# Recurrence levels in two groups of four matrix pairs instead of four groups of two

## What is computed

```
decay = jnp.exp(jnp.where(incl, gc[..., :, None] - gc[..., None, :], -jnp.inf))
lower = jnp.where(strict, bc[..., :, None] * kk * decay, 0.0)
sol = lax.linalg.triangular_solve(jnp.eye(CHUNK, dtype=f32) + lower, rhs, ...)
...
u = u_c - w_c @ S;  o = qd_c @ S + qk_c @ u;  S = exp(ge_c) * S + kd_c.T @ u
```

## Time and profile before

| | |
|---|---|
| median of 3 runs | 3671.87 us (3669.95 to 3673.09) |
| the profiled execution | 3669.49 us, its span 3667.7 us |
| busy in the span | PE 92%, PEld 76%, DVE 72%, ACT 53%, POOL 17% |
| mean granted TensorE clock | 0.957 of full speed |
| the recurrence | 284.7 to 565.0 us of the span |

### The profile page before, as it was taken

One profiled execution on the slowest core, in us unless ns is written; L12 is line 12 of the kernel. 1 busy time (PEld: TensorE's weight loads), 2 busy tenths in 40 slices (PEclk: granted clock), 3 DMA queues, 4 the chain that ended last, 5 costly groups with the idle time before them and its releaser, 6 DMA issues. The chain is left out here.

```text
span 3667.7 us, 46334 instructions
## 1 busy us (share of the span) xinstructions
PE 3362.4 (92%) x16708; PEld 2778.2 (76%) x16708; DVE 2648.5 (72%) x3181; ACT 1954.2 (53%) x2670; POOL 619.2 (17%) x605
## 2 busy tenths in 40 slices
PE   4998998998699999999999986888999988889999
PEld 2778997776588888888888873777787767768877
DVE  4777774965699999999999986786775246753323
ACT  4535543322588888888888863275322234743222
POOL 1006770000010101011010103184000013710000
PEclk8998999999799999999999997989999999999999
DMA  5318114852699999999999966501565322023322
GB/s 180 107 64 316 36 36 157 292 163 110 251 369 380 375 386 373 388 377 386 376 381 381 376 269 211 164 35 47 172 200 156 98 83 39 35 67 94 97 94 69
DMA packets 290590, 750.92 MB, mean 205 GB/s; under 512 B 35528, under 2 KB 161160, under 8 KB 237434
## 3 DMA queue, kind: packets, MB, share of 16 engines
q1 hardware_dynamic: 277068, 694.43, 52.5%
q0 software_dynamic: 8480, 36.71, 2.8%
q10 hardware_dynamic: 4896, 17.83, 1.2%
HBM read 697.40 MB, written 57.01 MB: 206 GB/s over the span
## 5 line engine op out<-in xcount | busy, mean ns | idle before, releaser
L2548 DVE TENSOR_TENSOR ex_WP_lo<-ex_W,ex_WP_hi 128x2048 fp32r<-128x2048 f32 x408 | 918.7, 2286 | 43.7 <-ACT ex_WP_hi L2472 39.2
L2472 ACT CAST ex_WP_hi<-ex_W 128x2048 fp32r<-128x2048 f32 x408 | 766.1, 1909 | 198.2 <-PE PS L73 173.5
L71 PE MATMUL PS<-ex_WP_hi,ex_xT_hi 128*128 128x512 f32 x1056 | 418.7, 396 | 11.2 <-DVE ex_xT_lo L2557 5.8
L73 PE MATMUL PS<-ex_WP_hi,ex_xT_lo 128*128 128x512 f32 x1056 | 412.5, 391 | 0.0
L72 PE MATMUL PS<-ex_WP_lo,ex_xT_hi 128*128 128x512 f32 x1056 | 412.0, 390 | 0.0
L2390 POOL COPY r_idc<-r_idx 128x1 uint32 x33 | 73.9, 2240 | 1044.7 <-PE PS L2403 1044.7
L71 PEld LDWEIGHTS PS<-ex_WP_hi,ex_xT_hi 128*128 128x128 f32 x1056 | 198.9, 188 | 64.3 <-issue 25.0
L71 PE MATMUL PS<-ex_WP_hi,ex_aT_hi 128*128 128x512 f32 x576 | 229.8, 399 | 10.1 <-DVE ex_aT_lo L2557 5.3
L73 PEld LDWEIGHTS PS<-ex_WP_hi,ex_xT_lo 128*128 128x128 f32 x1056 | 198.6, 188 | 42.2
L72 PEld LDWEIGHTS PS<-ex_WP_lo,ex_xT_hi 128*128 128x128 f32 x1056 | 199.0, 188 | 39.5
L73 PE MATMUL PS<-ex_WP_hi,ex_aT_lo 128*128 128x512 f32 x576 | 226.4, 393 | 0.0
(11 more groups left out here) (649 smaller groups left out, 8156.7 us busy)
## 6 DMA issues: line engine op xcount, KB each, us to landing
ex_W<-in_w_gate SPq DMA_DIRECT2D x136, 1024.0 KB, 7.2
ex_W<-in_w_up SPq DMA_DIRECT2D x136, 1024.0 KB, 7.7
ex_W<-in_w_down SPq DMA_DIRECT2D x136, 1024.0 KB, 8.0
ringb<-in_w_gu SPq DMA_DIRECT2D x88, 512.0 KB, 4.2
ringb<-in_w_mod SPq DMA_DIRECT2D x72, 512.0 KB, 4.6
ringa<-in_w_mod SPq DMA_DIRECT2D x56, 512.0 KB, 4.7
s_ybuf<-x_sb SPq DMA_DIRECT2D x3, 8192.0 KB, 26.5
ringb<-in_w_down SPq DMA_DIRECT2D x44, 512.0 KB, 3.3
```

What stands on the lines that cost most here:

```text
L71: nc.tensor.matmul(out, lhs.hi, rhs.hi, start=start, stop=False)
L73: return nc.tensor.matmul(out, lhs.lo, rhs.hi, start=False, stop=stop)
L2472: nc.scalar.copy(WP.hi[:, c % RP], W[:, c % RAW]).then_inc(s["hi"], 1)
L2548: nc.vector.tensor_tensor(WP.lo[:, c % RP], W[:, c % RAW], WP.hi[:, c % RP].bitcast(F32), ALU.subtract).then_inc(s["lo"][c % RP], 1)
```

## The change

The groups of a level become two of four head pairs, in banks 0 and 4: one wait, four matmuls (eight records) and one semaphore increment each. The copies to `Pm`, the subtractions, the block turns and the two copies behind the transposes cover 128x512 or 64x512 instead of 128x256 or 64x256, and there are half as many. TensorE's matmuls, their number and their order by head stay the same. GpSimd's masks stay at 128x256, two to a group, and TensorE waits for both. The transposes at level 5 go over banks 0 and 2, then 4 and 6. Semaphore counts follow, `Lm`'s index changes with the grouping, and at the start of a step fewer output banks are waited for.

```diff
-    PAIRS, W2, SIDE, HP = range(4), 2 * P, NV * P, P // 2
+    GR, W4, SIDE, HP = 2, 4 * P, NV * P, P // 2
...
         def Lm(i, lv, q):
             at = TOP * i + lv - 1
-            return (Lm1 if at % 2 else Lm0)[:, q, 2 * (at // 2 % 2):2 * (at // 2 % 2) + 2, :]
+            return (Lm1 if at % 2 else Lm0)[:, q + 2 * (at // 2 % 2), :, :]
...
-                for q in PAIRS:
+                for q, half in ((0, 0), (0, 1), (1, 0), (1, 1)):
...
-                        pool.wait_ge(s["pP"], 4 * (at - 4) + q + 1)
-                    nc.gpsimd.tensor_tensor(alike(Lm(n, lv, q), lv), straight(L(n), q, lv), alike(level_mask(lv), lv), ALU.mult).then_inc(s["lm"], 1)
+                        pool.wait_ge(s["pP"], GR * (at - 4) + q + 1)
+                    nc.gpsimd.tensor_tensor(alike(Lm(n, lv, q)[:, 2 * half:2 * half + 2, :], lv), straight(L(n), q, lv, half), alike(level_mask(lv), lv), ALU.mult).then_inc(s["lm"], 1)
...
-                    for q in PAIRS:
+                    for q in range(GR):
                         if lv == 1:
-                            pe.wait_ge(s["x0"], 4 * i + 2 + q // 2 + 1)
+                            pe.wait_ge(s["x0"], 4 * i + 2 + q + 1)
                             if i and want(i - 1):
-                                pe.wait_ge(s["oe"], m - 4 + q + 1)
+                                pe.wait_ge(s["oe"], m - 4 + 2 * q + 1)
                         else:
-                            pe.wait_ge(s["x"], 4 * (TOP * i + lv - 2) + q + 1)
+                            pe.wait_ge(s["x"], GR * (TOP * i + lv - 2) + q + 1)
...
-                        pe.wait_ge(s["lm"], 4 * (TOP * i + lv - 1) + q + 1)
-                        for j in range(2):
-                            last = nc.tensor.matmul(PS4[:, 2 * q, j, :], Lm(i, lv, q)[:, j, :], crossed(X(i), q, lv, j), start=True, stop=True)
+                        pe.wait_ge(s["lm"], 4 * (TOP * i + lv - 1) + 2 * q + 2)
+                        for j in range(4):
+                            last = nc.tensor.matmul(PS4[:, 4 * q, j, :], Lm(i, lv, q)[:, j, :], crossed(X(i), q, lv, j), start=True, stop=True)
...
-                    for q in PAIRS:
-                        pe.wait_ge(s["pm"], 4 * (TOP * i + lv - 1) + q + 1)
+                    for q in range(GR):
+                        pe.wait_ge(s["pm"], GR * (TOP * i + lv - 1) + q + 1)
...
-                        for j in range(2):
-                            last = nc.tensor.matmul(PS4[:, 2 * q, j, :], T[:, q, j, :], Pm[:, q, j, :], start=True, stop=True)
+                        for j in range(4):
+                            last = nc.tensor.matmul(PS4[:, 4 * q, j, :], T[:, q, j, :], Pm[:, q, j, :], start=True, stop=True)
...
-                            for j in range(2):
-                                for d in range(2):
-                                    last = nc.tensor.transpose(PS4[:, 2 * q, 2 * d + j, :], X(i)[:, 2 * d + q // 2, 2 * (q % 2) + j, :], g.ident[:, :])
+                            for d in range(2):
+                                for j in range(4):
+                                    last = nc.tensor.transpose(PS4[:, 4 * q + 2 * d, j, :], X(i)[:, 2 * d + q, j, :], g.ident[:, :])
...
-                        nc.scalar.copy(Pm[:, q, 0:2, :], PS4[:, 2 * q, 0:2, :]).then_inc(s["pm"], 1)
+                        nc.scalar.copy(Pm[:, q], PS4[:, 4 * q]).then_inc(s["pm"], 1)
...
-                            nc.scalar.copy(T[0:HP, q, 0:2, :], PS4[0:HP, 2 * q, 0:2, :]).then_inc(s["ta"], 1)
+                            nc.scalar.copy(T[0:HP, q], PS4[0:HP, 4 * q]).then_inc(s["ta"], 1)
...
-                nc.vector.transpose(alike(T[:, q, 0:2, :], lv), straight(X(n), q, lv)).then_inc(s["tv"], 1)
+                nc.vector.transpose(alike(T[:, q], lv), straight(X(n), q, lv)).then_inc(s["tv"], 1)
...
-                        nc.vector.tensor_tensor(crossed(X(i), q, lv), crossed(X(i), q, lv), alike(PS4[:, 2 * q, 0:2, :], lv), ALU.subtract).then_inc(s["x"], 1)
+                        nc.vector.tensor_tensor(crossed(X(i), q, lv), crossed(X(i), q, lv), alike(PS4[:, 4 * q], lv), ALU.subtract).then_inc(s["x"], 1)
...
-                            nc.vector.tensor_copy(T[HP:P, q, 0:2, :], PS4[HP:P, 2 * q, 2:4, :]).then_inc(s["tb"], 1)
+                            nc.vector.tensor_copy(T[HP:P, q], PS4[HP:P, 4 * q + 2]).then_inc(s["tb"], 1)
```

More of the change, by code:

```diff
@@ L1397, in crossed, with straight @@
         def crossed(tile, q, lv, j=None):
-            return halves(tile, q * W2, W2, lv, True) if j is None else halves(tile, q * W2 + j * P, P, lv, True)
-        def straight(tile, q, lv, j=None):
-            return halves(tile, q * W2, W2, lv, False) if j is None else halves(tile, q * W2 + j * P, P, lv, False)
+            return halves(tile, q * W4, W4, lv, True) if j is None else halves(tile, q * W4 + j * P, P, lv, True)
+        def straight(tile, q, lv, half=None):
+            return halves(tile, q * W4, W4, lv, False) if half is None else halves(tile, q * W4 + half * W4 // 2, W4 // 2, lv, False)
         def alike(v, lv):
@@ L1457, in part @@
                 at = TOP * n + lv - 1
-                for q in PAIRS:
+                for q, half in ((0, 0), (0, 1), (1, 0), (1, 1)):
                     if lv == 1:
-                        pool.wait_ge(s["L"], 16 * n + 8 + 2 * q + 2)
+                        pool.wait_ge(s["L"], 16 * n + 8 + 4 * q + 2 * half + 2)
                     if at >= 4:
-                        pool.wait_ge(s["pP"], 4 * (at - 4) + q + 1)
-                    nc.gpsimd.tensor_tensor(alike(Lm(n, lv, q), lv), straight(L(n), q, lv), alike(level_mask(lv), lv), ALU.mult).then_inc(s["lm"], 1)
+                        pool.wait_ge(s["pP"], GR * (at - 4) + q + 1)
+                    nc.gpsimd.tensor_tensor(alike(Lm(n, lv, q)[:, 2 * half:2 * half + 2, :], lv), straight(L(n), q, lv, half), alike(level_mask(lv), lv), ALU.mult).then_inc(s["lm"], 1)
             def from_identity(n):
@@ L1514, in _ @@
                     pool.dma_start(uT.hi[:, :, :], kept[0]).then_inc(s["back"][0], 16)
-            pool.wait_ge(s["pP"], 4 * TOP * NSTEP)
+            pool.wait_ge(s["pP"], GR * TOP * NSTEP)
             pool.dma_start(uT.lo[:, :, :], kept[1]).then_inc(s["back"][1], 16)
@@ L1573, in _ @@
                             turn(n, b)
[L1574 to L1575 removed]
+                    for q in range(GR):
+                        pe.wait_ge(s["pm"], GR * (TOP * i + lv - 1) + q + 1)
                         if lv < TOP:
[L1577 to L1579 removed]
+                            pe.wait_ge(s["tv"], GR * (LEAF * i + lv - 1) + q + 1)
+                        for j in range(4):
+                            last = nc.tensor.matmul(PS4[:, 4 * q, j, :], T[:, q, j, :], Pm[:, q, j, :], start=True, stop=True)
                         last.then_inc(s["pX"], 1)
@@ L1584, in _ @@
                     if lv == LEAF:
-                        for q in PAIRS:
-                            pe.wait_ge(s["x"], 4 * (TOP * i + lv - 1) + q + 1)
-                            for j in range(2):
-                                for d in range(2):
-                                    last = nc.tensor.transpose(PS4[:, 2 * q, 2 * d + j, :], X(i)[:, 2 * d + q // 2, 2 * (q % 2) + j, :], g.ident[:, :])
+                        for q in range(GR):
+                            pe.wait_ge(s["x"], GR * (TOP * i + lv - 1) + q + 1)
+                            for d in range(2):
+                                for j in range(4):
+                                    last = nc.tensor.transpose(PS4[:, 4 * q + 2 * d, j, :], X(i)[:, 2 * d + q, j, :], g.ident[:, :])
                             last.then_inc(s["pT"], 1)
                 for b, d, h in BT:
-                    pe.wait_ge(s["x"], 4 * (TOP * (i + 1) - 1) + b + 1)
+                    pe.wait_ge(s["x"], GR * (TOP * (i + 1) - 1) + b // 2 + 1)
                     if i:
@@ L1642, in _ @@
                 for lv in range(1, LEVELS):
-                    for q in PAIRS:
-                        act.wait_ge(s["pP"], 4 * (TOP * i + lv - 1) + q + 1)
-                        nc.scalar.copy(Pm[:, q, 0:2, :], PS4[:, 2 * q, 0:2, :]).then_inc(s["pm"], 1)
+                    for q in range(GR):
+                        act.wait_ge(s["pP"], GR * (TOP * i + lv - 1) + q + 1)
+                        nc.scalar.copy(Pm[:, q], PS4[:, 4 * q]).then_inc(s["pm"], 1)
                     if lv == LEAF:
-                        for q in PAIRS:
-                            act.wait_ge(s["pT"], 4 * i + q + 1)
-                            nc.scalar.copy(T[0:HP, q, 0:2, :], PS4[0:HP, 2 * q, 0:2, :]).then_inc(s["ta"], 1)
+                        for q in range(GR):
+                            act.wait_ge(s["pT"], GR * i + q + 1)
+                            nc.scalar.copy(T[0:HP, q], PS4[0:HP, 4 * q]).then_inc(s["ta"], 1)
                     if 2 <= lv <= LEAF and n < NSTEP:
@@ L1683, in block_turns @@
             def block_turns(n, q, lv):
```

(22 more changed lines are left out.)

4 lines of the change are left out of this document (2 added, 2 removed).

## The result

The changed kernel takes 3679.39 us in the median (3674.45 to 3680.49, 13 runs) against 3672.4 us before (3669.95 to 3673.9, 13 runs). The ratio is 1.0016, 95% interval 1.0009 to 1.0023. In a later comparison, on one chip, with 11 runs against 33, it was 1.0025 (1.0016 to 1.0034), with medians of 3680.34 and 3671.13 us. So the change makes the kernel slower, by 7 us between the medians of the first comparison and by 9 in the second.

A forecast was written before the change was run, and what follows sets the result against it. TensorE bounds the recurrence, and wider groups make round trips outlast its 1.79 us of own work. Terms over six steps sum to 7.7 us, which on the median of 3671.87 gives 3679.6 us, range 3673.5 to 3685.5.

The forecast's parts named there:

- P to X: Within a level: group result, ACT copy and wake-up take 1.86 us against 1.79 of TensorE's work, excess 0.06.
- X to P: Between levels: group result, DVE subtraction and wake-up take 1.96 us against 1.79 of TensorE's work, excess 0.16.
- step 0: First step, at a lower clock: first X takes 3.0 us and gives slack back; all terms together cost 1.25 us.
- The forecast's own term for this place: Steps 3 and 4, level 3: the copy held by E's load grows 0.23, earlier delays of 0.28 vanish.
- A level without cover: Levels 3, 4 and 5, with no other matmuls to hide the round trips: 0.22 us more each, 0.66 together.
- The leaf of step 5: Last step, from the transposes to level 6: 0.20 us more than the transposes' 1.75.
- Level 6: Subtractions queued on DVE before K*S: K*S starts 0.20 us later, 0.22 in step 5.
- X of step 1: Level 1 of step 1, no queries as cover: X waits for the longer first turn, 0.20 us in place of 0.06.
- Latency absorbed: Rival: slack or waits take up the delays, so the time stays within 0.2%, 3675 to 3676; chance 0.18.
- Work off ACT and DVE as the gain: Rival: fewer DVE and ACT instructions make it faster, 3671, or 3662 if all 10 us counted; chance 0.04, faster or equal.
- DVE as the bound: Rival: dearer turns make DVE limit levels 3 and 4; with dearer copies 3683.5 us; chance 0.16 for either.
- The clock: Rival: new gaps lower TensorE's clock, each step loses some 2.4 us, 3694 in all; chance 0.02.

The follow-up runs named there:

- e5: Kernel before with copies, subtractions and turns in three groups instead of four, leaf still in four; 3672.77 us against 3671.13, ratio 1.0002.
- e10: Changed kernel with the second direction of the next step's keys moved behind X of level 3; recurrence stretch 215.32 us against 215.96.
- e2: Kernel before with only DVE's subtractions (and X's groups) in two groups of four; recurrence stretch 214.63 us against 210.00.
- e7: Changed kernel with decay of the next step's last block ahead of the leaf's copies; recurrence stretch 212.89 us against 215.96, ratio to the kernel before 1.0013.
- e9: Kernel before with subtractions and turns in two groups of four, copies and leaf in four; recurrence stretch 213.95 us against 210.00.
- e3: Kernel before with only DVE's block turns in two groups of four; recurrence stretch 210.02 us against 210.00.
- e4: Kernel before with only the level 5 transposes and the copies behind them in two groups of four; recurrence stretch 212.37 us against 210.00.
- e6: Kernel before, groups unchanged, with decay of the next step's last block ahead of the leaf's copies; 3668.9 us against 3671.13, ratio 0.9992.
- e1: Kernel before with only ACT's copies (and P's groups) in two groups of four; recurrence stretch 211.79 us against 210.00.

## Why the prediction was right

**What bounds.** TensorE's halves stand back to back, and a round trip has 0.6 us of slack: shown by e5, where a part of the slack is used and its levels lose nothing, and by e10, where other work of TensorE in between takes the loss away.

**The unit costs.** Copy 0.585 us at the median (0.59), subtraction 0.687 (0.69), P to X is too long by 0.05 (0.06), X to P by 0.15 (0.16). The turn, which the trace lacked, lasts 0.69 and paces at 0.6, as the added elements had given.

**The steps.** From P to P, and in step 5 to K*S:

| | forecast | measured |
|---|---|---|
| step 0 | +1.25 | -0.18 |
| step 1 | +1.50 | +1.41 |
| step 2 | +1.30 | +1.17 |
| step 3 | +1.25 | +0.96 |
| step 4 | +1.25 | +1.26 |
| step 5 | +1.12 | +1.15 |
| steps 1 to 5 | 6.42 | 5.94 |

In steps 3 and 4 the waits at the load of `E` differ by -0.16 and +0.15; without them the steps are +1.12 and +1.11. The forecast's own term for this place (-0.28 + 0.23) is smaller than what varies there with the kernel unchanged, so it is neither shown nor refuted.

*Mis-sized terms.* A level without cover costs 0.20, not 0.22, which over three levels is 0.06 a step. The leaf of step 5 was to cost 0.20 and cost 0.31 (547.28 to 549.34, 2.06 instead of 1.75); the last section comes back to it. In steps 1 to 4 decay starts 2.51 after the first transpose (2.55 forecast), and the turns' wait shrinks from 1.53 to 1.42, so that the leaf costs 0.18 of the 0.22. Level 6 costs 0.18 (0.20); X of step 1 comes 0.25 late (0.20).

*Step 0.* This term failed as a whole, though most of it did not. From level 2's P on, step 0 loses 1.06, where the same terms of the forecast make 1.14. But its first P and X took 5.14 us together instead of 6.37: X alone took 1.95 instead of 3.0, near its length at the full clock, 1.79. This does not follow the grouping. The first X took 3.0 to 3.1 us before and in e2, e7 and e9, and 1.8 to 2.0 in all other profiles, e3, e4 and e6 with their narrow copies among them. Over the step the granted clock was 0.89 in the changed kernel's profile and 0.87 before. The forecast took the slow first X of one profile as given.

**What the sum left out.** The two profiled spans differ by 10.9 us. Up to K*S of step 5 it is 6.3, of which 0.55 lies ahead of step 0's first P. Here is the rest of both kernels from one place on, in the last fifth of the span, with the same 3074 loads:

```profile
2961.00:3667.70 706.70, 646.47 (x3074) 531.78 (x3074) 337.29 (x611) 273.42 (x496) 127.58 (x127) 0.96 0.24 71
```

```profile
2968.60:3678.60 710.00, 648.39 (x3074) 530.65 (x3074) 338.96 (x611) 273.67 (x496) 128.59 (x127) 0.96 0.24 71
```

3.3 us differ there, in code that the change doesn't touch, and 1.2 between the two places. Counted from the first of these loads, the span's rest takes 706.1 us before, 706.2 in e9 and 706.3 in e3. In all other profiles it takes 708.8 to 709.5, in e6 with its narrow groups too. So it comes in two lengths, and e9, with wide subtractions and turns, has the short one: this part isn't the grouping's doing. What sets it was not tried. The medians differ by 7.0 and in the later comparison by 9.2 us, steps 1 to 5 by 6; whether the remaining 1 to 3 us are all of this kind stays open. That the forecast of 3679.6 comes so close to 3679.39 is in part luck. It added 7.7 us to a median of three runs, 3671.87; the thirteen runs have 3672.4, and the difference is 7.0. Within the 7.7, step 0 was 1.4 too high and the other steps 0.5, and something behind the recurrence made up for it.

**The rivals.** Latency absorbed: falls (e4; the wait at the turns moves along with the transposes). Work off ACT and DVE as the gain: falls (e1, e2); where DVE is late, in e2, two instructions fewer for a level's turns do give time back (e9). DVE as the bound: not in the changed kernel, where it still idles 0.21 us before the second subtraction of levels 4 and 5, but true in small in e1 and e2, where its turns were left in four; I had worked it out only for dearer turns. The clock stays at 1.00 in steps 1 to 5.

The Trainium skill (VectorE: DVE Perf Modes, "The TRN2 errata") gives 691 ns for an fp32 add of 512 elements, against 687 for the subtraction here. Its advice to make tiles of 512 elements or more is given for instructions that read SBUF; the copies here read PSUM, and the subtractions both. Followed here, it cost 5.96 us, although DVE and ACT were busy for less time. A wide instruction also starts later and ends later, and TensorE waits for the first group's result and not for DVE's total.

## What to carry to other kernels

Where an engine goes round with others in groups, compare two times: what one group takes for its result, the copy and the wake-up, and the engine's own work for all groups. As long as the first fits into the second, width cost nothing here (e5); the first group size that didn't fit cost the excess on every round without cover. Fewer, wider instructions paid only where the narrow ones' engine was what the others waited for (e9 against e2). Look for that level by level: a mean over the step hid that DVE had 3.66 us of work in a level of 3.57. Where a wait was the end of a chain of several links, an edit of their order (e6, 3.26 us) was worth more than the link's size in this kernel.

## What was not expected of the hardware

- **A load behind separate waits starts later.** At level 6, P waits for both halves of the leaf's copies, the mask and the subtraction. DVE's copy ends at 357.66 + 0.69 = 358.35, and the load starts at 358.58, 0.23 later, where elsewhere it is 0.05. The bracket says "issue". The trace has two waiting instructions of 0.05 each on TensorE's queue in front of this load, at 358.39 and 358.50, and the load follows 0.03 after the second. In the kernel before, such instructions lie among the last transposes (one at 356.61), and the load starts at 356.84 without an idle time. That they make up the 0.23 is how I read it; no run takes them away.
- **The load of E.** The same kernel waits 0.84 and 1.11 us in step 4 in two profiles, and over all twelve profiles the sum over steps 2 to 4 runs from 1.5 to 4.3 us. What sets the landing was not tried.
